# Modulation sums of the second layer: ones-column products on TensorE in place of transposes and ScalarE accumulations

## The reference

```
mod_lat = (jax.nn.silu(c) @ w_mod[i] + b_mod[i])[:, None, :]
mod_ctx = (jax.nn.silu(c_ctx) @ w_mod[i] + b_mod[i])[None, None, :]
sh1, sc1, gt1, sh2, sc2, gt2 = jnp.split(mod_lat, N_MOD, axis=-1)
h = modulate(rms_norm(x_lat, g_norm1[i]), sh1, sc1)      # h * (1 + sc1) + sh1
```

## Time and profile before

| | |
|---|---|
| median of 3 runs | 1839.16 us (1836.52 to 1845.0) |
| the profiled execution | 1836.52 us, of which the span 1834.7 us |
| mean granted clock of TensorE | 0.98 |
| busy: PE, PEld, DVE, ACT, POOL | 1754.6, 1427.0, 1106.6, 899.9, 459.6 us |

### The profile page before, as it was taken

One profiled execution on the slowest core, in us unless ns is written; L12 is line 12 of the kernel. 1 busy time (PEld: TensorE's weight loads), 2 busy tenths in 40 slices (PEclk: granted clock), 3 DMA queues, 4 the chain that ended last, 5 costly groups with the idle time before them and its releaser, 6 DMA issues.

```text
span 1834.7 us, 28671 instructions
## 1 busy us (share of the span) xinstructions
PE 1754.6 (96%) x10708; PEld 1427.0 (78%) x10708; DVE 1106.6 (60%) x1971; ACT 899.9 (49%) x1933; POOL 459.6 (25%) x864
## 2 busy tenths in 40 slices
PE   6998999899999998989899989999999899999998
PEld 3452454588888885737899989899899898998998
DVE  3328841688878633383555577577555585785555
ACT  2326631443444433373555566576454475675542
POOL 1016001000000001150000026048772152286730
PEclk8998989899999999999999999999999999999999
DMA  8520631255555530301355542633345335333351
GB/s 289 181 92 2 229 138 46 92 184 183 184 184 184 184 93 26 138 1 47 138 184 184 184 152 92 229 139 105 127 154 183 133 141 184 138 139 113 126 196 50
DMA packets 140020, 255.26 MB, mean 139 GB/s; under 512 B 14942, under 2 KB 21740, under 8 KB 139884
## 3 DMA queue, kind: packets, MB, share of 16 engines
q1 hardware_dynamic: 138886, 251.16, 38.9%
q0 software_dynamic: 704, 2.10, 0.3%
q10 hardware_dynamic: 294, 0.18, 0.0%
HBM read 252.38 MB, written 1.05 MB: 138 GB/s over the span
## 4 chain that ended last, share of the span: by engine, by line
PE 91%; DVE 5%; ACT 2%; issue 1%; DMA 1%; POOL 0%; SPq 0%; DVEq 0%; ACTq 0%; POOLq 0%
PE ps L1158 18%; PE ps L1160 18%; PE ps L1159 18%; PE ps L1183 10%; PE ps L1043 2%; PE ps L1299 2%; PE ps L1398 2%; PE ps L1399 2%; PE ps L1400 2%; PE ps L1325 2%; PE ps L1311 1%; PE ps L1114 1%; PE ps L1070 1%; PE ps L1478 1%; PE ps L1481 1%
## 5 line engine op out<-in xcount | busy, mean ns | idle before, releaser
L1587 ACT ACTIVATE big_r<-ring 128x1024 fp32r<-128x1024 f32 x198 | 209.1, 1058 | 355.4 <-PE ps L1160 342.0
L2021 DVE TENSOR_TENSOR big_r<-ring,big_r 128x1024 fp32r<-128x1024 f32 x198 | 245.1, 1239 | 218.6 <-ACT big_r L1587 218.4
L1159 PE MATMUL ps<-big_r 128*128 128x256 f32 (+1 forms) x1088 | 360.6, 331 | 0.0
L1158 PE MATMUL ps<-hT_r,big_r 128*128 128x256 f32 (+1 forms) x848 | 270.4, 319 | 0.0
L1160 PE MATMUL ps<-hT_r,big_r 128*128 128x256 f32 (+1 forms) x848 | 265.6, 313 | 0.0
L910 POOL TENSOR_TENSOR sq<-sq 128x256 f32<-128x256 f32 (+1 forms) x30 | 36.5, 1218 | 765.1 <-ACT sq L1547 765.1
L1159 PEld LDWEIGHTS ps<-big_r 128*128 128x128 f32 x1088 | 206.8, 190 | 18.7
L1183 PE MATMUL ps<-hT,ring 128*128 128x512 f32 (+1 forms) x544 | 191.9, 513 | 11.1 <-ACT hT L1608 9.5
L1158 PE MATMUL ps<-big_r 128*128 128x256 f32 (+1 forms) x592 | 196.3, 332 | 1.4 <-DVE big_r L2181 1.4
L1160 PE MATMUL ps<-big_r 128*128 128x256 f32 (+1 forms) x592 | 194.8, 329 | 0.0
L1183 PEld LDWEIGHTS ps<-hT,ring 128*128 128x128 f32 x544 | 105.3, 195 | 94.9 <-issue 80.2
(11 more groups left out here) (315 smaller groups left out, 4203.4 us busy)
## 6 DMA issues: line engine op xcount, KB each, us to landing
ring<-in_w_in SPq DMA_DIRECT2D x42, 2048.0 KB, 7.8
ring<-in_w_mlp SPq DMA_DIRECT2D x32, 2048.0 KB, 7.6
ring<-in_w_mod SPq DMA_DIRECT2D x24, 2048.0 KB, 7.9
ring<-in_w_out SPq DMA_DIRECT2D x4, 2048.0 KB, 7.7
ring<-in_w_out_a SPq DMA_DIRECT2D x4, 2048.0 KB, 8.6
ring<-in_w_out_b SPq DMA_DIRECT2D x4, 2048.0 KB, 7.7
ring<-in_w_o SPq DMA_DIRECT2D x4, 2048.0 KB, 8.2
ring<-in_w_in SPq DMA_DIRECT2D x12, 256.0 KB, 4.7
```

The source lines that it names most:

```text
L1158: mm(b[:, 0:T], w_hi[:, k, :], hi(k), start=(k == 0), stop=False)
L1159: mm(b[:, 0:T], w_hi[:, k, :], lo(k), start=False, stop=False)
L1587: act_fn(hi, raw, ACT.Copy).then_inc(hi_ready, 1)
L2021: V.tensor_tensor(lo, raw, hi.bitcast(F32), ALU.subtract).then_inc(lo_ready, 1)
```

## The change

The two transposes and the two ACT reductions of a slot are taken away. In their place `late_sum(j)` on PE makes, for each of the four pieces and both conditionings, one product with the piece of `mod_acc` as weights and one column of ones as moving data. That sums over the partitions and puts the 128 results on the partitions. All 96 results of the 12 slots lie in one bank (bank 3, key `modsum`) in columns of their own, so that the bank is taken once and given free once. `late_sum(j - 1)` stands after the fourth granule of slot `j`. DVE's wait for the free half of `mod_acc` goes to a new counter, `acc_used`. The bias is added by `mod_biased`, straight from the bank, after granule (12, 3).

```diff
@@ -239,9 +239,7 @@
         for m in range(FF // P):
             take((tag, "up", m), m % 3)
         if i == 0:
-            for j in range(N_LATE):
-                for s in range(2):
-                    take((tag, "late", j, s), 3)
+            take((tag, "modsum"), 3)
         for n in range(BLOCKS):
             for m in range(KC):
                 take((tag, "down", n, m), 4 + m % 4)
@@ -559,6 +557,7 @@
         silu_tanh = sem("silu_tanh")
         silu_made = sem("silu_made")
         acc_ready = sem("acc_ready")
+        acc_used = sem("acc_used")
         late_used = sem("late_used")
         modA_made = sem("modA_made")
         modB_made = sem("modB_made")
@@ -628,7 +627,7 @@
 
         def await_acc_free(eng, j):
 
-            await_bank(eng, (("a", 0), "late", j, 1))
+            eng.wait_ge(acc_used, j + 1)
 
         def gain(s, row, rows=P):
             return prm[0:rows, s, row:row + 1]
@@ -1127,14 +1126,20 @@
                 if n1 == end:
                     fill(last, key)
 
-            def late_transposed(j, s):
-
-                key = (("a", 0), "late", j, s)
-                b = start_bank(key)
+            def late_sum(j):
+
+                key = (("a", 0), "modsum")
+                b = start_bank(key) if j == 0 else bank(key)
                 pe.wait_ge(acc_ready, 2 * (j + 1))
                 for m in range(4):
-                    last = tr(b[:, m * P:(m + 1) * P], mod_acc[:, j % 2, s, m * P:(m + 1) * P], IDENT)
-                fill(last, key)
+                    for s in range(2):
+                        col = 2 * (4 * j + m) + s
+                        last = mm(b[:, col:col + 1], mod_acc[:, j % 2, s, m * P:(m + 1) * P], cc("ones", P, 1),
+                                  start=True, stop=True)
+                if j == N_LATE - 1:
+                    fill(last, key)
+                else:
+                    last.then_inc(acc_used, 1)
 
 
             source = [None]
@@ -1353,7 +1358,7 @@
                         if (j, m) == (0, 0):
                             split_products_in_step(n, lambda k: h_hi[:, k, t0:TOK], lambda k: h_lo[:, k, t0:TOK], TOK - t0)
                         elif (j, m) == (0, 1):
-                            pass
+                            continue
                         elif name == "up":
                             split_product(n, lambda k: h_hi[:, k, t0:TOK], lambda k: h_lo[:, k, t0:TOK], TOK - t0)
                         else:
@@ -1361,8 +1366,8 @@
 
                                 source[0] = (up_ready, n // 16 * KC, 1)
                             split_product(n, lambda k: hid_hi[:, k, t0:TOK], lambda k: hid_lo[:, k, t0:TOK], TOK - t0)
-                        if i == 0 and 1 <= j <= N_LATE and m % 2:
-                            late_transposed(j - 1, m // 2)
+                    if i == 0 and 1 <= j <= N_LATE:
+                        late_sum(j - 1)
 
 
             pe.wait_ge(consts_made, 2)
@@ -1608,15 +1613,6 @@
                         act_fn(hT[:, k, s * SEQ:(s + 1) * SEQ], nt[:, k % 2, s * SEQ:(s + 1) * SEQ], ACT.Identity,
                                bias=mod[:, i, which + k, s:s + 1]).then_inc(h_ready, 1)
 
-            def late_reduced(j, s):
-
-                key = (("a", 0), "late", j, s)
-                await_bank(act, key)
-                for m in range(4):
-                    last = act_fn(pb[:, 0, m * P:(m + 1) * P], bank(key)[:, m * P:(m + 1) * P], ACT.Copy,
-                                  accum_out=mod[:, 1, 4 * j + m, s:s + 1])
-                drain(last, key)
-
             def run_units(tag, units):
                 n = len(units)
                 for j in range(n + MS_LAG):
@@ -1728,9 +1724,6 @@
                         await_drained(act, key)
                         link(act_fn(f, f, ACT.Square))
                         act_fn(hid_hi[:, k, t0:TOK], f, ACT.Copy).then_inc(hid_ready, 1)
-                    j, q = divmod(g - g0, 4)
-                    if i == 0 and 1 <= j <= N_LATE and q % 2:
-                        late_reduced(j - 1, q // 2)
 
             exps = sum(24 * len(sets_of(j)) for j in range(DEPTH))
             for l in range(DEPTH):
@@ -2187,11 +2180,9 @@
                     j, q = divmod(g - g0, 4)
                     if i == 0 and j < N_LATE:
                         late_partial(j, q)
-                    if i == 0 and (j, q) == (N_LATE + 1, 0):
-
-                        bias = prm[:, 1, RA["b_mod"]:RA["b_mod"] + 48].unsqueeze(2).to_broadcast([P, 48, 2])
-                        await_drained(dve, (tag, "late", N_LATE - 1, 1))
-                        link(V.tensor_tensor(mod[:, 1, :, :], mod[:, 1, :, :], bias, ALU.add))
+                    if i == 0 and (j, q) == (N_LATE, 3):
+
+                        mod_biased(1, 0, 48, ("modsum",))
                         mod_scaled(1, 8, RA["g1"], 0, modA_made)
                         mod_scaled(1, 32, RA["g2"], 1, modB_made)
```

## The result

The changed kernel takes 1848.47 us (median of 8 runs, 1844.7 to 1850.18) against 1839.09 us for the kernel before (8 runs, 1836.39 to 1845.0). The ratio is 1.0058, 95% interval 1.0042 to 1.0074: slower, by 7.7 to 13.6 us. The forecast was 1839.7 us and the range 1834 to 1845 us. The prediction was wrong.

The account below looks back on a forecast made before the run. PE was taken to bound the kernel: -11.5 us for transposes and +12.0 us for products on PE, nothing elsewhere, gave +0.5 us on the 1839.2 us median, so 1839.7 us; range 1834 to 1845 us.

Parts of the forecast that it names:

- The bound: From 365 to 650 us PE is busy throughout at full clock and never waits; only PE's stream counts.
- What goes on ACT: 96 copies and 96 accumulator reads, 44.5 us, leave ACT; valued at 0 because ACT waits for PE there.
- What goes on PE: 24 groups of four transposes leave PE's stream, 0.48 us each, 11.5 us in all.
- What comes on PE: 12 groups of eight products join PE's stream, 0.114 us a product, 1.0 us a group, 12.0 us.
- The waits: Moved waits of PE for `mod_acc` and DVE for `acc_used`, and the bias after granule (12, 3), cost 0.
- Columns: Rival: moved columns set a product's price on PE, 0.60 us a group, -4.3 us, 1834.9 us; chance 0.12.
- hidden loads: Rival: PE loads weights ahead, so groups cost only the join, -10.5 us, 1828.7 us; chance 0.04.
- The clock: Rival: each group of eight sets off a fall of PE's clock to half, +22 us, 1862 us; chance 0.04.
- The pace is worse inside the stream: Rival: clock stays up, but products take 0.22 us with a 0.2 us join, +12.2 us, 1851.4 us; chance 0.02.
- No full-clock row has it: Argument against the worse pace on PE: no trace row at full clock shows products at 0.22 us.
- The upper bound of the sum: +12.2 us on PE, from the half-clock pace of 0.22 us a product and a 0.2 us join.
- DVE's wait on the new counter: Rival: DVE waits for `acc_used`, some tenths of a us in 11 places, 1840 us; chance 0.02.

Follow-up runs that it names:

- b_noact: The kernel before with each of ACT's 24 reductions cut to a copy of four columns, sums left out: 1838.59 us, ratio 0.9997.
- b_plain: The kernel before with its 96 transposes made ordinary f32 products with the identity: 1849.88 us, ratio 1.0063.
- a_f32r: The changed kernel with DVE's last sum and the ones written as fp32r, two moving columns instead of one: 1839.92 us, ratio 0.9998.
- strips: The changed kernel with operands swapped: 32-column weights with one column of ones, accumulator moving in four strips of 32 partitions side by side: 1837.18 us, ratio 0.9994.
- wide: The changed kernel with two fp32r products a slot, 128-column selector weights, accumulator moving 512 columns, summed in one bank: 1836.12 us, again 1835.06 us, ratio 0.9976 both times.

## Why the prediction was wrong

*The bound.* Right: PE is the bound of this stretch before and after, and nothing else in the stretch came to the path.

*What goes on ACT.* Valued at 0, right (b_noact). Its size was wrong: 24.0 us and not 44.5, since I added the busy times of the copies and of the reads, which overlap, the very mistake that I avoided for PE. In order of time on ACT, in the kernel before:

```profile
379.60 0.26 ACT L1616 ACTIVATE pb<-ps 128x128 f32<-128x128 f32 x1
379.76 0.19 ACT L1616 ACTIVATION_READ_ACCUMULATOR pb<-ps 128x1 f32 x1
379.85 0.27 ACT L1616 ACTIVATE pb<-ps 128x128 f32<-128x128 f32 x1
```

A pair starts 0.25 us after the one before it, and 96 x 0.25 = 24.0 us.

*What goes on PE.* 11.5 us, right; b_noact has the same step.

*What comes on PE.* This step failed, and alone carries the error. It read "48 of them take 265.11 - 259.62 = 5.49 us, 0.114 us each" as 48 products; they are 24 products in 48 records. The term was 12 x 1.0 = 12.0 us and measured 22.2. Its other parts hold: 0.114 us a record, hardly any price for the join (0.02 us, I took 0.08), 12 groups. With 16 x 0.114 in the place of 8 x 0.114 the same working gives 1.83 + 0.08 = 1.91 us a group, 22.9 us, +11.4 us. The trace of before would have told: 96 records at L1126 against 48 instructions.

Nor does a record stand for one passage of the columns. The kernel before has a stream of f32 products with 512 columns at the full clock:

```profile
116.12 13.90 PE L1183 MATMUL ps<-hT,ring 128*128 128x512 f32 x32
```

The 32 records are two calls of `plain_product` with eight products each, again two a product. Less the last one's tail (0.59 us), 31 starts in 13.31 us are 0.429 us a record, so 0.86 us a product, 3.8 times the 0.2267 us of an fp32r product with as many columns.

The Trainium skill bears on this on a page that I did not weigh (FP8 and Floating Point Precision, section TensorE Precision Notes): a true FP32 product takes four passes through the array, high and low halves crosswise. The trace agrees in the price at 512 columns (3.8) and shows the four as two records. At up to 128 columns the price is only that of two records, 0.23 us a product, where a transpose takes 0.11. The Trainium skill also says (Perfetto Trace Analysis, section Transposes) to use the transpose and not a standard matmul for a transpose; b_plain puts 10.2 us on it here.

*The waits.* Right: DVE did not wait for the last group, and no wait of PE stands in the stretch.

*The rivals.* Columns and hidden loads fell: a record costs about 0.114 us, whether it moves one column (after, 1.846 / 16 = 0.115), two (a_f32r, 0.953 / 8 = 0.119 with the join) or 128 (b_plain, 0.907 / 8 = 0.113). The clock stayed at 1.00. "The pace is worse inside the stream" named 0.22 us a product and 1851.4 us, the nearest figure, and had 0.02; its place was right, its reason (a pace that only half clock shows) was not. "No full-clock row has it" was false by the same miscount. The upper bound of the sum, +12.2 us, takes in the measured +10.6, but by luck: it rests on the same half-clock row, whose 0.22 us a record happens to lie near the 0.229 us of two records at full clock. DVE's wait on the new counter did not show at all in the list of waits.

*The chances.* 0.06 for slower rested on a unit price I held for measured. It was measured, but in records, and the count of what was added was in instructions.

## What to carry to other kernels

Before a row of the trace prices an instruction, hold its record count against the program's count of that line; f32 products count double here, transposes and fp32r products once. For products with full weights and up to 128 columns the number of records sets the price here, not the columns moved; at 512 columns the columns do (0.429 us a record in f32). Where PE is the bound, try a reduction over partitions in the shape of the products beside it. Of the five forms measured here (transposes and ACT, f32 and fp32r products with ones as moving data, strips, wide) it was the cheapest: one column of ones in the weights, the data as moving columns, everything added up in one bank.

## What the runs showed of the hardware that I had not expected

In a full stream a transpose with 128 moving columns costs the same as one record of a product with 128 x 128 weights and 1 to 128 moving columns, 0.11 us. Four strips of 32 partitions, 256 columns each, ran eight records in 0.57 us at the full clock, but the steps before and behind them are 0.32 and 0.33 us instead of 0.227, and a group cost the stream 0.80 us in all. An fp32r product of 512 columns with other weights and another bank joins the stream at 0.24 us a piece, nearly its own step.
